# Turning mixer A's probabilities of the sample tiles without TensorE: 32x32 block transposes on VectorE and 16 DMAs per tile

## The reference

```python
s = jnp.einsum('bqhcd,bshcd->bhcqs', qb, k).astype(jnp.float32) * scale   # c: two score maps per head
p = jax.nn.softmax(s, axis=-1)
p = p[:, :, 0] - lam[None, :, None, None] * p[:, :, 1]
return jnp.einsum('bhqs,bshe->bqhe', p.astype(v.dtype), v)
```

## Time and profile before

| | |
|---|---|
| time, median of 3 runs | 1254.29 us (1253.92 to 1254.44) |
| profiled execution, span | 1253.5 us; the profile gives no other time of it, and the median lies 0.8 us above its span |
| PE busy | 98% |
| DVE, ACT, POOL busy | 64%, 49%, 21% |
| mixer A's transposes of sample tiles | 8 heads x 4 tiles x 6 = 192 |

### The profile page before, as it was taken

How to read it: one execution, slowest core, us unless ns; L and a number is a source line. 1 busy time by engine, 2 the same in 40 slices (tenths; PEclk the granted TensorE clock), 3 DMA queues, 4 the chain that set the end, 5 groups by cost and what they waited for, 6 DMA issues and landing times.

```text
span 1253.5 us, 16906 instructions
## 1 busy us (share of the span) xinstructions
PE 1222.7 (98%) x6251; PEld 991.3 (79%) x6251; DVE 800.0 (64%) x1242; ACT 619.1 (49%) x1296; POOL 258.3 (21%) x439
## 2 busy tenths in 40 slices
PE   5899999999999999999999999999999999999996
PEld 3455778888888888888888888888888888888885
DVE  4455488667586776755546374554647675789774
ACT  5522325645555465565556555656556765312223
POOL 1211033012031040222221221222223322211111
PEclk9999999999999999999999999999999999999998
DMA  9999242222221232322222121222224423756544
GB/s 348 371 377 349 84 110 76 62 71 74 76 96 44 67 106 53 100 60 83 71 61 86 51 91 51 82 59 83 59 72 133 139 83 98 254 187 228 184 135 177
DMA packets 130482, 156.45 MB, mean 125 GB/s; under 512 B 8304, under 2 KB 97040, under 8 KB 129632
## 3 DMA queue, kind: packets, MB, share of 16 engines
q1 hardware_dynamic: 116528, 109.60, 26.7%
q0 software_dynamic: 13424, 45.20, 11.4%
q10 hardware_dynamic: 448, 0.57, 0.1%
HBM read 144.18 MB, written 11.16 MB: 124 GB/s over the span
## 4 chain that ended last, share of the span: by engine, by line
PE 92%; SPq 3%; DVE 2%; DMA 1%; ACT 1%; POOL 1%; issue 0%; POOLq 0%; DVEq 0%; ACTq 0%
PE z_ps L704 24%; PE z_ps L706 23%; PE z_ps L705 23%; PE ring L795 5%; PE ring L884 4%; SPq L658 2%; PE ring L829 2%; PE ring L828 2%; PE ring L730 2%; PE ring L888 2%; DMA ada_raw<-in_w_ada_dram 1%; PE ring L706 1%; PE ring L705 1%; PE ring L891 1%; PE ring L704 1%
## 5 line engine op out<-in xcount | busy, mean ns | idle before, releaser
L704 PE MATMUL z_ps<-w_hi,xt_hi 128*128 128x512 f32 x1350 | 554.1, 410 | 2.6 <-issue 1.1
L706 PE MATMUL z_ps<-w_hi,xt_lo 128*128 128x512 f32 x1350 | 527.7, 391 | 0.0
L705 PE MATMUL z_ps<-w_lo,xt_hi 128*128 128x512 f32 x1350 | 527.2, 391 | 0.0
L1007 ACT ACTIVATE w_hi<-w_raw 128x512 fp32r<-128x512 f32 x270 | 169.3, 628 | 334.9 <-PE z_ps L706 309.2
L704 PEld LDWEIGHTS z_ps<-w_hi,xt_hi 128*128 128x128 f32 x1350 | 254.0, 188 | 68.1 <-issue 27.2
L1441 DVE TENSOR_TENSOR w_lo<-w_raw,w_hi 128x512 fp32r<-128x512 f32 x270 | 196.8, 732 | 162.6 <-ACT w_hi L1007 162.2
L706 PEld LDWEIGHTS z_ps<-w_hi,xt_lo 128*128 128x128 f32 x1350 | 253.4, 188 | 55.3
L705 PEld LDWEIGHTS z_ps<-w_lo,xt_hi 128*128 128x128 f32 x1350 | 254.8, 189 | 38.8
L1542 DVE TENSOR_REDUCE small<-s_sb 128x2 f32<-128x1536 f32 (+1 forms) x60 | 87.6, 1460 | 20.6 <-ACT s_sb L1007 20.6
L1153 ACT ACTIVATE s_sb<-s_sb,small 128x768 f32<-128x768 f32 (+1 forms) x120 | 98.0, 821 | 3.6 <-DVE small L1542 3.5
L1902 POOL TENSOR_TENSOR sg<-sg,zs 128x128 f32<-128x128 f32 (+1 forms) x60 | 38.6, 644 | 276.2 <-DVE sg L1511 275.6
(11 more groups left out here) (196 smaller groups left out, 1378.3 us busy)
## 6 DMA issues: line engine op xcount, KB each, us to landing
w_raw<-in_w_in_dram SPq DMA_DIRECT2D x188, 256.0 KB, 3.1
ada_raw<-in_w_ada_dram SPq DMA_DIRECT2D x64, 512.0 KB, 11.6
w_raw<-in_w_out_dram SPq DMA_DIRECT2D x64, 256.0 KB, 3.8
gate_raw<-in_w_ada_dram POOLq DMA_DIRECT2D x12, 1024.0 KB, 8.0
w_raw<-in_w_in_dram POOLq DMA_DIRECT2D x20, 256.0 KB, 6.3
o_spill<-row_st POOLq DMA_DIRECT2D x14, 320.0 KB, 3.4
row_st<-o_spill POOLq DMA_DIRECT2D x14, 320.0 KB, 3.3
x_sb<-in_x_sample_dram SPq DMA_DIRECT2D x4, 1024.0 KB, 9.6
```

The costliest lines, as they stand in the source:

```text
L704: pe.matmul(out, hi_l, hi_r, start=start, stop=False)
L705: pe.matmul(out, hi_l, lo_r, start=False, stop=False)
L706: return pe.matmul(out, lo_l, hi_r, start=False, stop=stop)
L1007: return act.activation(out, in_, ACT.Copy, **kw)
```

## The change

For the sample tiles of mixer A step T is gone from PE. ACT writes the scores with the keys in another order, in four groups of 32. DVE, when it has combined the two maps, transposes 32x32 blocks into the free half of the buffer. These stay in their quarter of the partitions, and SP moves them to their place with 16 DMAs of 32 partitions x 768 bytes, into one of two new tiles `pt_t`. V waits for all 16 and takes every sixth element of a row of `pt_t` as its stationary operand (24 bytes apart). The turned blocks leave DVE as runs of one element, 24 bytes apart too. Tile 0 keeps its one transpose on PE.

```diff
     if kind == "T":
-        return (2 if t else 1) * (2 if g == "G" and t else 1)
+        return 0 if t and g == "D" else 4 if t else 1
...
+    pt_t = [place(f"pt_t{i}", [P, P, KB], F32, pt0 + 4 * NKEY * i)[0] for i in range(2)]
...
+        def quads(row):
+            return row.rearrange("p (i k b) -> p k i b", i=QUAD, b=P // QUAD)
...
+            def turn_blocks(a, t):
+                b = t % 2
+                sp.wait_ge(p_turned, (TILES - 1) * (a - D_IT) + t)
+                if t > 2:
+                    wait_full(sp, TURN[("V", a, t - 2)])
+                else:
+                    wait_full(sp, TURN[("V", a - 1, t + 2 if group_kind(a - 1) == "D" else TILES - 1)])
+                w = P // QUAD
+                for i in range(QUAD):
+                    for j in range(QUAD):
+                        sp.dma_start(pt_t[b][w * i:w * (i + 1), w * j:w * (j + 1), :].rearrange("a q k -> a (q k)"),
+                                     s_sb[w * j:w * (j + 1), b, 1, w * KB * i:w * KB * (i + 1)]).then_inc(pt_in[b], 16)
+            j = EARLY_PAIRS
+            for q, (it, s) in enumerate(ORDER):
+                turns = [(a, t) for kind, a, t in (steps_at(*ORDER[q - 1]) if q else []) if kind == "S" and t and group_kind(a) == "D"]
+                if turns:
+                    while j <= min(q // 2 + 3, len(ORDER) // 2 - 1):
+                        load_w(sp, j)
+                        j += 1
+                for a, t in turns:
+                    turn_blocks(a, t)
...
# PE, step_v
+                if t and group_kind(a) == "D":
+                    pe.wait_ge(pt_in[t % 2], 16 * QUAD * QUAD * p_count(a, t))
-                        ins = pe.matmul(bank[:, 0:DH], pt_f[:, keys], v_f[:, vt, :],
+                        ins = pe.matmul(bank[:, 0:DH], pt_t[t % 2][:, :, j] if t else pt_f[:, :], v_f[:, vt, :],
...
# ACT, scores_out of a sample tile (before: two copies of 512 and one of both rests)
+                    if t > 2:
+                        act.wait_ge(pt_in[t % 2], 16 * QUAD * QUAD * p_count(a, t - 2))
+                    for c_ in range(2):
+                        wait_full(act, n + c_)
+                        copy(quads(s_sb[:, t % 2, c_, :])[:, 0:LAT], RB(n + c_)[:, :].rearrange("p (k i b) -> p k i b", k=LAT, i=QUAD),
+                             scale=DK_A ** -0.5).then_inc(free_sem(n + c_), 1)
+                    wait_full(act, n + 2)
+                    for c_ in range(2):
+                        ins = copy(quads(s_sb[:, t % 2, c_, :])[:, LAT:],
+                                   RB(n + 2)[:, 256 * c_:256 * (c_ + 1)].rearrange("p (k i b) -> p k i b", k=PAST, i=QUAD),
+                                   scale=DK_A ** -0.5)
...
# DVE, combine
+                if t:
+                    dve.wait_ge(p_ready, m + 1)
+                    dve.transpose(e2.rearrange("p (i b k) -> p i k b", i=QUAD, k=KB), e1.rearrange("p (i k b) -> p i k b", i=QUAD, k=KB)).then_inc(p_turned, 1)
```

More of the change, by code:

```diff
@@ L434, in build @@
         pt_hi_done = sem("pt_hi_done")
+        p_turned = sem("p_turned")
+        pt_in = [sem(f"pt_in{b}") for b in range(2)]
         o_part, o_sq, o_rstd, og_ready = sem("o_part"), sem("o_sq"), sem("o_rstd"), sem("og_ready")
@@ L537, in t_parts, with p_count @@
                 return [(n, c, 0, 1, P * c, c == heads(a) - 1) for c in hs]
+            if group_kind(a) == "D":
+                return []
             return [(n + 2 * c + j // 4, c, j, m, 0, True) for c in hs for j, m in ((0, 4), (4, 2))]
+        def p_count(a, t):
+            return 2 * (a - D_IT) + (t - 1) // 2 + 1
+        def quads(row):
+            return row.rearrange("p (i k b) -> p k i b", i=QUAD, b=P // QUAD)
         PT_BEFORE = {}
@@ L673, in _ @@
                 load_ada(n)
-            for j in range(EARLY_PAIRS, ITS * KT // 2):
+            def turn_blocks(a, t):
[19 more added lines that the diff above has]
+                    turn_blocks(a, t)
+            for j in range(j, ITS * KT // 2):
                 load_w(sp, j)
@@ L1127, in scores_out @@
                     act.wait_ge(zr_ready, a + 1)
-                if group_kind(a) == "D":
+                if group_kind(a) == "D" and t == 0:
+                    if a > D_IT:
+                        act.wait_ge(pt_in[0], 16 * QUAD * QUAD * p_count(a - 1, 4))
                     for c_ in range(2):
                         wait_full(act, n + c_)
-                        kn = 512 if t else P
-                        copy(s_sb[:, t % 2, c_, 0:kn], RB(n + c_)[:, 0:kn],
+                        copy(s_sb[:, 0, c_, 0:P], RB(n + c_)[:, 0:P],
                              scale=DK_A ** -0.5).then_inc(free_sem(n + c_), 1)
[L1134 to L1137, removed]
+                    return
+                if group_kind(a) == "D":
+                    if t > 2:
+                        act.wait_ge(pt_in[t % 2], 16 * QUAD * QUAD * p_count(a, t - 2))
+                    elif t == 1 and a > D_IT:
+                        act.wait_ge(pt_in[1], 16 * QUAD * QUAD * p_count(a - 1, 3))
+                    for c_ in range(2):
[7 more added lines that the diff above has]
+                                   scale=DK_A ** -0.5)
+                    ins.then_inc(free_sem(n + 2), 1)
                     return
```

3 lines of the change are left out of this document (2 added, 1 removed).

## The result

The changed kernel takes 1358.26 us (median of 4 runs, 1352.14 to 1358.82) against 1254.37 (1253.92 to 1254.48) for the kernel before: a ratio of 1.082, with a 95% interval of 1.0799 to 1.0841. It is 104 us slower, where 7 us less was forecast and 23 us more was the end of the range.

The account below looks back on a forecast made before the run. PE, busy 98% of the span, was taken as the bound: -21.1 (transposes) + 0 (loads) + 9 + 5 (waits) = -7 us, giving 1247 us; range 1236 to 1277 for 8 in 10.

Parts of the forecast that it names:

- Term 1: PE's transposes removed: six a tile at 0.11 us each, 0.66 us a tile, 21.1 us off the path for 32 tiles.
- Term 2: V's 384 weight loads on PE, now reading every sixth element: nothing added, 0 us.
- The upper bound: V's strided weight loads at twice the columns' time: 0.107 us more a record, 1.28 us a tile, 41 us in all.
- The rival with strided loads: V's weights come in at half the rate: +39 us, waits shrink to some 3, 1275 us in all; chance 0.29.
- at +0.02 us a record: Extra time per V weight load at which 384 loads use up the 7 us of forecast gain.
- Term 3 (c): SP's issue of a tile's 16 DMAs: 0.455 us from start to start (0.41 to 0.48), 7.3 us a tile.
- Waits at V of tile 1 to 3 in normal heads: Sign in PE's profile that would say issue or landing is longer than taken; only tile 4 was expected to wait there.
- The rival of the long turnaround: Transpose, issue and landing at upper ends: PE waits 3.7 us in seven heads, 8 in the last, 1267 us; chance 0.10.
- Term 3 (b): DVE's transpose of 768 elements a partition: 1.02 us, as long as the combination needs for as many.
- Term 3 (d): Landing of a tile's 24 KB DMA blocks, SBUF to SBUF: 1.9 us.
- What was queued behind the waits: Work behind SP's issues and ACT's wait: weight loads 2 to 3 us late, 5 in the last head, all hidden.

Follow-up runs that it names:

- parts 1 and 4: Changed kernel with plain loads 1355.12 us, four DMAs a tile 1283.48, both 1248.73; then with 8-byte load steps 1360.07, DMAs on two queues 1293.28, both 1262.53.

## Why the prediction was wrong

**Term 1, the transposes: right.** 192 records fewer, and six heads without them gain 13.6 us against 6 x 2.64 = 15.8; 288 loads of V at 196 instead of 191 ns take back 1.4 of the difference.

**Term 2, the loads: the step that failed first.** "I take nothing added" came from the transposes' loads at 140 ns, by which "the reading side can thus deliver twice what V's loads ask for". The load takes 317 ns, 125 more, V 1.22 us more a tile without a wait before it and 1.41 behind one: 45 us in all. The upper bound, 0.107 us a record and 1.28 a tile, 41 us, was about the truth. The inference was bad in its kind: the 140 ns are those of loads of neighbouring elements, and say nothing of elements 24 bytes apart. The rival with strided loads, 0.29, had the mechanism and the size; its condition, "at +0.02 us a record", was passed more than five times over (0.111). The expectations of parts 1 and 4 reckon with 0.239 us between V's records and 49 or 47 us; that was read from the duration of a V behind a wait, and is some 4 to 8 us too much.

**Term 3 (c), the issues: the step that failed worst.** The price was taken as 0.455 us from start to start, with 0.48 as its upper end, from weight DMAs in pairs, between which SP rested, and two small ones of ACT. A tile's issues take 0.63 to 0.64 each (durations of 0.59). Worse than the price was the shape of the sum: one tile's chain was followed to its V, and SP was asked only whether it was late for that tile. Nobody added up the queue. At the forecast's own price four tiles are 4 x 7.3 = 29 us and three pairs of weights 3 more, with transpose and landing 35 of the 36.8 us that the stretch has: nearly full already. At the real price it is 48. So each tile is later than the one before it, and most V's wait, the sign that the forecast itself had named for it ("Waits at V of tile 1 to 3 in normal heads"). The rival of the long turnaround (1267) had the right kind of mechanism but added up single tiles, with the issue at 0.48 at most: the waits came to 59 us of idle PE, not 34, and to the clock on top.

**Term 3 (b), the transpose: mis-sized.** 1.02 us was taken, between 0.49 and 1.74; it measured 1.62, and 0.98 where it writes in steps of 8 bytes. The rival named the 24-byte steps as its suspicion, rightly.

**Term 3 (d), the landing: right.** 1.8 us against 1.9.

**What was queued behind the waits: half missed.** "`scores_out` of tile 3 now waits for tile 1's DMAs, about when they land" was dismissed as hidden. This wait (ACT's, for `pt_t`'s DMAs that still read `s_sb`) closes the loop in which a late SP delays ACT's scores, these the maximum, the exponentials and the next transpose, and so SP again; 19.7 us of PE's idle time stand under its name.

**The clock: not in the sum.** The forecast counted waits at their face value. In the changed kernel the lower level came with them, 14 us of work at half pace beside 59 us of waits, and where the loads were cheap it also doubled the V behind a long wait (1.58 us to 2.90).

**The sum with its terms as measured**: -21 + 45 + 59 + 14 + 5 = +102, of +104.

## What to carry to other kernels

When a change adds instructions to a queue, add up what that queue has to do between the first and the last of its readers, at the price of issues that directly follow each other, before following one tile's chain: a queue that is full there is a floor, and under a floor no other saving shows. Keep the float32 elements that a weight load reads in a row no more than 8 bytes apart: 128 of them took 196 ns at 8 bytes, 261 at 12, and 315 to 329 from 16 to 24. Where the last turns of a loop share their queues with other work and have no slack for the new chain, leave the change out of them: six heads of eight gave 1.0%, eight lost 0.65%.

## What the runs showed of the hardware that was not expected

- A load of 128 float32 weights takes 192, 196, 261, 329, 315 and 317 ns for steps of 1 to 6 elements at a granted clock of 1.00.
- At the lower level, a granted clock of 0.50, the load with a step of 1 takes some 333 ns, but that with a step of 6 stays at 317: the lower clock costs that load nothing.
- An issue of a turned tile's DMA on SP takes 0.59 to 0.62 us directly behind another one, 0.51 behind a pause, against a median of 0.436 for the weight DMAs before; POOL's eight in a row take 0.50 (rows of 768 bytes) or 0.55 (three pieces of 256 bytes) each. Why was not found; it isn't the shape of the rows, and it isn't how many follow (4, 8 and 16 have the same 0.59).
- With 16 DMAs of 24 KB a tile, it is not the landing that bounds here, at 1.8 us, but the issues, 10 us a tile.
- The 32 x 32 transpose of 768 float32 a partition on DVE: 0.98 us with output steps of 8 bytes, 1.62 with 24.
- DMAs of 96 KB (four a tile) behind 1.75 MB of other loads took up to 10.5 us to land, elsewhere 2.1 in the median; with the big loads moved away none took over 4.5.
